# Four expert groups in turn, and the final norm of all rows under the last expert block

## The chip, the cores and the metric

One core of a Trainium2 chip runs the kernel. The metric is the device time of one execution in microseconds. Three runs of the kernel before gave 2179.16, 2179.3 and 2180.51, a median of 2179.3.

## The reference, cut to what matters

Two transformer-like blocks follow each other. What the change touches is the end of the second: a mixture of experts with 32 experts in 4 groups of 8, and the last norm.

```python
g_idx = argmax(g_logits)                       # one of 4 groups for each of 1024 tokens
top_val, top_loc = lax.top_k(e_logits, 2)      # two experts of that same group
expert = g_idx * 8 + top_loc
dest = pad_starts[expert] + rank               # sorted by expert, each padded to blocks of 128
out = (silu(xb @ w_gate[e]) * (xb @ w_up[e])) @ w_down[e]    # one block, one expert
y = zeros.at[slot_tok].add(out * slot_gate)    # rows go back to their tokens
x = x + gate_f * y
return rms_norm_2(x, final_g)                  # every row
```

Sums over experts may be made in any order, so the order of the blocks is free. Blocks of one expert never share a token; a token's two experts are always in one group.

## The kernel before, in words

The second block's residual rows lie in DRAM as `x3_dram`, the normed rows as `h4_dram`. Routing is worked out on VectorE (DVE, lines 1935 to 2070) with a few matmuls: one-hot vectors over 32 experts in `hot32`, their counts, slots, and for each block its expert (`bexp_u[:, 0]`), read by SyncE (SP) into a register when it loads weights. The last entry of `bexp` is the number of blocks beyond 32; its arrival raises `ov_known`. Blocks stand in the order of the experts, group after group.

Each block takes 12 weight chunks of 512 KB through a ring of 12 slots in SBUF. Matmuls are float32 made of three passes: ScalarE (ACT) copies a chunk to a rounded high part `mH`, DVE subtracts it from the chunk to get the low part `mL` (L2043 in the main loop, L2112 in the overflow blocks), and TensorE (PE) multiplies high by high, low by high and high by low (L2156, L2157, L2159). When a chunk's subtraction is done (`m2_lo`), its ring slot is free and SP loads the next block's chunk into it.

GpSimd (Pool) gathers a block's rows (L839, in the overflow blocks L906), and scatters the finished rows of the block before by an accumulating DMA into `x3_dram` (L850). A scatter waits until the scatter before has landed. The rows come out of PSUM by ACT, scaled by the slot's gate (L1305 and L1347), and Pool multiplies them by the modulation row `gate_ffn_row` (L844).

32 blocks are a fixed loop. The blocks beyond (here three) run in `overflow_blocks`: every engine walks 15 turns of a loop and skips the body where there is no block. In turn b the block 32 + b is computed, and the output of the block before it is weighed and scattered. In DVE's queue the body is: a small copy of row numbers (L2109), 12 subtractions (L2112), the hidden product (L2118), its low part (L2122), the low part of the next block's rows (L2127). PE waits for the hidden product's transposes before the down products.

Behind the loop the last block's rows are scaled by ACT (L1369), gated by Pool in two halves, and scattered. SP waits for that scatter (`last_out`), loads the 8 row tiles of `x3_dram` (L616), ACT squares them with a running sum (L1374), DVE makes the variance (L2134), Pool the power -0.5 (L935), DVE the scaled row times the final gain (L2139), and SP stores the tile (L619). Inputs go to `mH` and `mL`, squares and outputs to the ring.

Of the kernel before, what the change touches and what calls it, by code (L numbers as in the profile page):

```python
# [6 lines left out]
F32 = mybir.dt.float32  # L7
# [5 lines left out]
P = 128  # L13
D = 1024
# [20 lines left out]
    q_mm pm_ready pv hn_tr num_out final_in dve_steps cols_tr mod_mm xn_done  # L35
    tr_lo sums_out sums2_out sums_in row_cols row_tr row_copied rows_out rows_here c_here mid_tr tr_mid v_mm pool_steps neg_out mb_in mask_done exp_done small_ready small_exp sq_out intra_out kt_mm kw_out st_mm c_ready hd_out cell_w ov_l last_y last_out m2_row m2_dst rows_known aff_ready halves_out affT_tr m1_xT_lo m1_hid m1_hT_lo if_lo v_odd if_mm pool_mm k_mm k_out s_mm
    hn_ready q_out
# [46 lines left out]
def build(nc, ctx, io, out):  # L84
    def sb(name, shape, dt=F32, scope=ctx):
        return scope.enter_context(nc.sbuf_tensor(name, shape, dt))
# [104 lines left out]
    cnt_u = sb("cnt_u", [P, E2], U32, moe)  # L191
    bexp = sb("bexp", [P, NBLK + 1], scope=moe)
    bexp_u = sb("bexp_u", [P, 2, NBLK + 1], U32, moe)
    final_row = sb("final_row", [P, D], scope=moe)
# [50 lines left out]
    for name in SEMS.split():  # L245
# [5 lines left out]
        [("x1_done", NT), ("x1_done_2", NT)],  # L251
        [("sq2", NT), ("sq2_2", NT), ("sq_final", NT)],
        [("var2", NT), ("var2_2", NT), ("var_final", NT)],
        [("rstd2", NT), ("rstd2_2", NT), ("rstd_final", NT)],
        [("h2_out", 16 * NT), ("h2_out_2", 16 * NT)],
# [98 lines left out]
    def settle(eng):  # L354

        eng.sem_inc(S["wait_passed"])
# [55 lines left out]
    def m2_steps(eng, body):  # L412
# [6 lines left out]
        for s in range(E2 - 2, E2 + 1):  # L419
            body(s // 2, s % 2)  # L420

    def overflow_blocks(eng, overflow):
# [10 lines left out]
    one_rows = [ring[:, 2 * t, :] for t in range(6)] + [xz[:, 6, :], sg]  # L433
    two_rows = [ring[:, 2 * t + 1, :] for t in range(6)] + [xz[:, 7, :], hid]
    x_rows = [(mH, mL)[t // WSETS][:, t % WSETS, :].bitcast(F32) for t in range(NT)]
    row_at = [{}, {}]
# [15 lines left out]
    def _(sp):  # L452
# [157 lines left out]

        overflow_blocks(sp, overflow)


        sp.wait_ge(S["last_out"], 16)
        for t in range(NT):
            sp.dma_start(x_rows[t], x3_tiles[:, t, :]).then_inc(x_in[t], 16)  # L616
        for t in range(NT):
            sp.wait_ge(S["final_done"], t + 1)
            sp.dma_start(out.rearrange("(t p) d -> p t d", p=P)[:, t, :], one_rows[t]).then_inc(x_in[t], 16)  # L619
        for t in range(NT):  # L620
# [4 lines left out]
    def _(pool):  # L625
# [277 lines left out]
        def overflow(b):  # L903
            pool.wait_ge(S["ov_tok"], b + 1 + past["ov_tok"])
            settle(pool)
            pool.indirect_dma_start(out=xs[0], out_offset=None, in_=h4_dram,  # L906
                                    in_offset=bass.IndirectOffsetOnAxis(ap=otok[:, 0:1], axis=0),
                                    bounds_check=T - 1, oob_is_err=False).then_inc(xs_in[0], 16)
            pool.wait_ge(S["ov_y"], b + 1 + past["ov_y"])
            settle(pool)  # L910
            pool.wait_ge(m2_out[1], 16 * (E2 // 2 - 1) + XS_PAST)
            pool.wait_ge(m2_out[0], 16 * b + 16 * (E2 // 2) + XS_PAST)
# [5 lines left out]
            pool.wait_ge(S["m2_row"], 2 * b + 3 * (E2 - 1) + 2)  # L918
            settle(pool)
# [3 lines left out]
        pool.wait_ge(m2_out[1], 16 * (E2 // 2 - 1) + XS_PAST)  # L923
        pool.wait_ge(m2_out[0], 16 * blocks + 16 * (E2 // 2) + XS_PAST)
        settle(pool)
        pool.tensor_copy(last_tok[:], row_of[:, bass.ds(blocks + (E2 - 1), 1)]).then_inc(S["m2_row"], 1)
        for half in range(2):
            pool.wait_ge(S["last_y"], half + 1)
            gate_rows(ys[0], ys[0], slice(512 * half, 512 * half + 512))
        pool.wait_ge(S["m2_row"], 2 * blocks + 3 * (E2 - 1) + 3)  # L930
        settle(pool)
        scatter_rows(ys[0], last_tok).then_inc(S["last_out"], 16)
        for t in range(NT):
            pool.wait_ge(S["var_final"], t + 1 + past["var_final"])
            pool.tensor_tensor(stat[:, 10, t:t + 1], stat[:, 9, t:t + 1], neghalf[:, 0:1], ALU.pow).then_inc(S["rstd_final"], 1)  # L935


    @block.scalar
    def _(act):
# [399 lines left out]
        def overflow(b):  # L1339
            used, hi = past["m2_used"] + 12 * E2, past["m2_xT_hi"] + 2 * E2  # L1340
            for c in range(12):
                if c == 6:
                    act.wait_ge(S["m2_used"], 12 * b + used)
                    act.wait_ge(m2_out[1], 16 * (E2 // 2 - 1) + XS_PAST)
                    act.wait_ge(S["m2_row"], 2 * b + 3 * (E2 - 1))
                    settle(act)
                    act.activation(ys[1].rearrange("p (a b) -> p a b", a=2), ps[:, 4:6, :], ACT.Copy,  # L1347
                                   scale=slot_w[:, bass.ds(b + (E2 - 1), 1)]).then_inc(S["ov_y"], 1)
                if c == 9:
# [14 lines left out]
        blocks = overflow_blocks(act, overflow)  # L1364
        act.wait_ge(m2_out[0], 16 * (E2 // 2) + XS_PAST)
        act.wait_ge(S["m2_used"], 12 * blocks + 12 * E2 + past["m2_used"])
        settle(act)
        for half in range(2):
            act.activation(ys[0][:, 512 * half:512 * half + 512], ps[:, 4 + half, :], ACT.Copy,  # L1369
                           scale=slot_w[:, bass.ds(blocks + (E2 - 1), 1)]).then_inc(S["last_y"], 1)  # L1370

        for t in range(NT):
            act.wait_ge(x_in[t], 48)
            act.activation(two_rows[t], x_rows[t], ACT.Square,  # L1374
                           accum_out=stat[:, 8, t:t + 1]).then_inc(S["sq_final"], 1)


    @block.vector
    def _(dve):
# [724 lines left out]
        m2_steps(dve, m2_step)  # L2104

        def overflow(b):
# [22 lines left out]

        overflow_blocks(dve, overflow)  # L2130

        def variance(t):
            dve.wait_ge(S["sq_final"], t + 1 + past["sq_final"])
            dve.tensor_scalar(stat[:, 9, t:t + 1], stat[:, 8, t:t + 1], 1.0 / D, EPS, ALU.mult,  # L2134
                              ALU.add).then_inc(S["var_final"], 1)

        def finish(t):
            dve.wait_ge(S["rstd_final"], t + 1 + past["rstd_final"])
            dve.scalar_tensor_tensor(out=one_rows[t], in0=x_rows[t], scalar=stat[:, 10, t:t + 1], in1=final_row[:],  # L2139
                                     op0=ALU.mult, op1=ALU.mult).then_inc(S["final_done"], 1)  # L2140

        dve.wait_ge(S["final_in"], 16)
        for t in range(NT):
            variance(t)
            if t:
                finish(t - 1)
        finish(NT - 1)


# [567 lines left out]
```

## Time and profile before

| what | us |
|---|---|
| median of three runs | 2179.3 |
| the profiled execution's own time | 2180.93 |
| its span | 2179.3 |
| PE busy | 2030.7 (93%) |
| DVE busy | 1672.9 (77%) |
| ACT busy | 1240.9 (57%) |
| Pool busy | 467.9 (21%) |
| mean granted clock of PE | 0.973 |

The span is the time between the first and the last instruction of the profiled execution; the own time of that execution has what lies around the span too. An engine's busy time says how full it is, not whether it is what others wait for; for that one looks at what it waits for itself, and at the chain of work that ended last. The main expert loop of the second block lies between about 1505 and 2064 us, the three overflow blocks between 2064 and 2144, the last norm behind.

### The profile page before, as it was taken

What the parts mean: (1) busy time and instruction counts of PE and PEld (TensorE: products, weight loads), DVE (VectorE), ACT (ScalarE), POOL (GpSimd) and SP (SyncE); (2) the same over time, 40 slices, a digit from 0 to 9 for tenths busy, and PEclk for the clock granted to TensorE, in tenths of its full rate; (3) what the DMA queues carried; (4) which work ended last, traced back from release to release, by engine and by line L of the source; (5) the groups of instructions that cost most, each with busy time, mean ns of one, the idle gap of its engine ahead of it and who ended that gap; (6) DMA issues with size and microseconds to landing.
All of it is one profiled execution on the core that took longest, in us unless ns stands there. A gap on an engine that the chain in (4) does not pass through costs nothing.

```text
span 2179.3 us, 32240 instructions
## 1 busy us (share of the span) xinstructions
PE 2030.7 (93%) x9821; PEld 1685.3 (77%) x9821; DVE 1672.9 (77%) x1890; ACT 1240.9 (57%) x1460; POOL 467.9 (21%) x367
## 2 busy tenths in 40 slices
PE   3999999969999999999699999999999999999993
PEld 2888888857888878787577787888888888878872
DVE  5676755478999999999545455447999999999994
ACT  4311103207878787877533533223888888888873
POOL 2000001101011111111100353110344443433443
PEclk9999999959999999999899999999999999999997
DMA  9277754528999999999711112345999999999994
GB/s 344 89 249 242 244 189 165 198 102 317 381 378 389 380 387 381 386 382 385 262 44 47 41 39 106 126 174 192 395 382 383 376 370 379 377 374 365 367 333 155
DMA packets 234180, 592.47 MB, mean 272 GB/s; under 512 B 23938, under 2 KB 61078, under 8 KB 234108
## 3 DMA queue, kind: packets, MB, share of 16 engines
q1 hardware_dynamic: 207808, 518.06, 63.8%
q0 software_dynamic: 22640, 61.31, 9.6%
q10 hardware_dynamic: 3660, 12.17, 1.5%
q8 instruction: 42, 0.69, 0.1%
q14 instruction: 30, 0.25, 0.0%
HBM read 560.57 MB, written 50.91 MB: 281 GB/s over the span
## 4 chain that ended last, share of the span: by engine, by line
PE 50%; DMA 23%; DVE 11%; SPq 6%; issue 5%; ACT 3%; POOL 1%; ACTq 0%; DVEq 0%; POOLq 0%
PE ps L2156 15%; PE ps L2159 14%; PE ps L2157 14%; DMA ring<-in_w_expert_up 13%; DMA ring<-in_moe_w_down 7%; SPq L534 5%; DVE mL L2043 2%; DVE mL L1646 2%; DMA ring<-in_ada_w 1%; ACT mH L1292 1%; PE ps L2291 1%; PE ps L2435 1%; DVE xz L1792 1%; PE ps L2164 1%; PE ps L2253 1%
## 5 line engine op out<-in xcount | busy, mean ns | idle before, releaser
L2043 DVE TENSOR_TENSOR mL<-ring,mH 128x1024 fp32r<-128x1024 f32 x384 | 480.0, 1291 | 25.1 <-ACT mH L1292 24.4
L1646 DVE TENSOR_TENSOR mL<-ring,mH 128x1024 fp32r<-128x1024 f32 x384 | 454.8, 1222 | 33.8 <-ACT mH L1107 25.2
L1107 ACT ACTIVATE mH<-ring 128x1024 fp32r<-128x1024 f32 x384 | 402.2, 1063 | 100.8 <-PE ps L2159 61.2
L1292 ACT ACTIVATE mH<-ring 128x1024 fp32r<-128x1024 f32 x384 | 398.6, 1058 | 64.7 <-DMA ring<-in_w_expert_up 32.1
L2156 PE MATMUL ps<-mH,xsH 128*128 128x512 f32 x1072 | 428.7, 400 | 4.1 <-DVE mL L2043 2.4
L2159 PE MATMUL ps<-mH,xsL 128*128 128x512 f32 x1072 | 419.3, 391 | 0.0
L2157 PE MATMUL ps<-mL,xsH 128*128 128x512 f32 x1072 | 417.4, 389 | 0.0
L2156 PEld LDWEIGHTS ps<-mH,xsH 128*128 128x128 f32 x1072 | 201.6, 188 | 44.0 <-issue 3.3
L2159 PEld LDWEIGHTS ps<-mH,xsL 128*128 128x128 f32 x1072 | 201.2, 188 | 43.7
L2157 PEld LDWEIGHTS ps<-mL,xsH 128*128 128x128 f32 x1072 | 201.7, 188 | 38.7
L2156 PE MATMUL ps<-mH,hidH 128*128 128x512 f32 x536 | 213.6, 399 | 9.9 <-DVE hidL L1691 7.4
L844 POOL TENSOR_TENSOR xz<-xz,gate_ffn_row 128x340 f32<-128x340 f32 (+3 forms) x98 | 164.0, 1678 | 251.3 <-DVE mL L2043 210.3
L2157 PE MATMUL ps<-mL,hidH 128*128 128x512 f32 x536 | 209.7, 391 | 0.0
L2159 PE MATMUL ps<-mH,hidL 128*128 128x512 f32 x536 | 165.9, 391 | 0.0
L2156 PE MATMUL ps<-hH,wH 128*128 128x512 f32 x384 | 151.7, 395 | 3.8 <-DVE hL L1448 3.3
L2157 PE MATMUL ps<-hL,wH 128*128 128x512 f32 x384 | 150.0, 391 | 0.0
L2156 PEld LDWEIGHTS ps<-mH,hidH 128*128 128x128 f32 x536 | 100.9, 188 | 35.3 <-DVE mL L1646 11.3
L717 POOL DMA_INDIRECT xz<-h_dram,tok_in x16 | 42.8, 2675 | 376.8 <-DVE tok_in L1656 376.8
L1392 DVE SCALAR_TENSOR_TENSOR acc<-ring,silu_c,acc 128x1024 f32<-128x1024 f32 x83 | 106.6, 1284 | 22.1 <-DMA ring<-in_ada_w 15.1
L2159 PE MATMUL ps<-hH,wL 128*128 128x512 f32 x384 | 122.7, 391 | 0.0
L2159 PEld LDWEIGHTS ps<-mH,hidL 128*128 128x128 f32 x536 | 101.2, 189 | 21.8
L2157 PEld LDWEIGHTS ps<-mL,hidH 128*128 128x128 f32 x536 | 101.0, 188 | 19.5
(419 smaller groups left out, 3187.2 us busy)
## 6 DMA issues: line engine op xcount, KB each, us to landing
ring<-in_w_expert_gate SPq DMA_DIRECT2D x140, 512.0 KB
ring<-in_w_expert_up SPq DMA_DIRECT2D x140, 512.0 KB
ring<-in_w_expert_down SPq DMA_DIRECT2D x140, 512.0 KB
ring<-in_moe_w_gate SPq DMA_DIRECT2D x128, 512.0 KB
ring<-in_moe_w_up SPq DMA_DIRECT2D x128, 512.0 KB
ring<-in_moe_w_down SPq DMA_DIRECT2D x128, 512.0 KB
ring<-in_ada_w SPq DMA_DIRECT2D x96, 512.0 KB
ring<-in_sc_w_in SPq DMA_DIRECT2D x24, 512.0 KB
```

What stands on the lines that cost most here:

```text
L534: sp.dma_start(dst, src).then_inc(ring_in[s], 16)
L717: pool.indirect_dma_start(out=xs[r], out_offset=None, in_=h2_dram, in_offset=bass.IndirectOffsetOnAxis(ap=tok_in[r][:, 0:1], axis=0)).then ...
L844: pool.tensor_tensor(dst[:, at], src[:, at], gate_ffn_row[:, at], ALU.mult).then_inc(S["m2_row"], 1)
L1107: act.activation(mH[:, m % WSETS, :], ring[:, m % RING, :], ACT.Copy).then_inc(S["m1_hi"], 1)
L1292: act.activation(mH[:, wset, :], ring[:, slot, :], ACT.Copy).then_inc(S["m2_hi"], 1)
L1392: ins = dve.scalar_tensor_tensor(out=acc[:], in0=slot, scalar=silu_c[:, silu_col + k:silu_col + k + 1], in1=acc[:], op0=ALU.mult, op1=ALU.add)
L1646: dve.tensor_tensor(mL[:, m % WSETS, :], ring[:, m % RING, :], mH[:, m % WSETS, :].bitcast(F32), ALU.subtract).then_inc(S["m1_lo"], 1)
L1792: ins = dve.scalar_tensor_tensor(out=xz[:, i, back:T], in0=tA[:, 0:T - back], scalar=col("conv_w_2", 4 * (3 - back) + i), in1=xz[:, i, bac ...
L2043: dve.tensor_tensor(mL[:, wset, :], ring[:, slot, :], mH[:, wset, :].bitcast(F32), ALU.subtract).then_inc(S["m2_lo"], 1)
L2156: pe.matmul(o, high, rh, start=start, stop=False)
L2157: pe.matmul(o, high, rl, start=False, stop=False)
L2159: last = pe.matmul(o, low, rh, start=False, stop=stop)
```

## The change

It has four parts.

1. *Order of the blocks.* The one-hot vectors are written with a step of 4, so that place 4 * l + g holds expert l of group g. Four more DVE steps turn the place back into the expert's number, before `ov_known` is raised.
2. *Overflow blocks.* The weighing of the block before moves from ACT and Pool to one DVE instruction, ahead of the sixth subtraction. DVE then waits for `ov_sent`, a semaphore that Pool raises behind its scatter instruction. Pool no longer gates; it waits for the scatters before and scatters.
3. *Final norm of all rows under the last block.* SP waits for the scatter of the last block but one and for the ring slots of the last block, and then loads the 8 tiles of `x3_dram` to ring slots 0 to 7. Tiles are squared to ring slots 8 to 11, finished in place and stored as before.
4. *The last block's rows are patched in.* Pool gathers their rows of `x3_dram` (which lack the last block only); DVE weighs the last block's output and adds them; they pass the same norm as a ninth tile; when all eight stores have landed, Pool scatters these rows over `out`.

```diff
-                steps.mark(dve.tensor_tensor(hot32[:, i, :, 8 * g:8 * g + 8], hot8[:, i],
+                steps.mark(dve.tensor_tensor(hot32[:, i, :, bass.ds(g, 8, step=4)], hot8[:, i],
...
-        steps.mark(dve.tensor_copy(bexp_u[:, 0, 0:NBLK], bexp[:, 0:NBLK]))
+        step(dve.tensor_copy(bexp_u[:, 0, 0:NBLK], bexp[:, 0:NBLK]))
+        step(dve.tensor_scalar(bexp_u[:, 1, 0:NBLK], bexp_u[:, 0, 0:NBLK], 3, None, ALU.bitwise_and))
+        step(dve.tensor_copy(bgrp[:], bexp_u[:, 1, 0:NBLK]))
+        step(dve.scalar_tensor_tensor(out=bexp[:, 0:NBLK], in0=bgrp[:], scalar=31.0, in1=bexp[:, 0:NBLK], op0=ALU.mult,
+                                      op1=ALU.add))
+        steps.mark(dve.tensor_scalar(bexp_u[:, 0, 0:NBLK], bexp[:, 0:NBLK], 0.25, None, ALU.mult))
```

SP, behind the overflow blocks:

```diff
-        sp.wait_ge(S["last_out"], 16)
+        sp.wait_ge(m2_out[0], 16 * (E2 // 2) + XS_PAST)
+        sp.wait_ge(m2_out[1], 16 * blocks + 16 * (E2 // 2 - 1) + XS_PAST)
+        settle(sp)
         for t in range(NT):
+            sp.wait_ge(S["m2_lo"], 12 * blocks + 12 * (E2 - 1) + t + 1 + past["m2_lo"])
+            settle(sp)
             sp.dma_start(x_rows[t], x3_tiles[:, t, :]).then_inc(x_in[t], 16)
```

Pool, in each overflow block and behind them:

```diff
+            pool.wait_ge(m2_out[0], 16 * (E2 // 2) + XS_PAST)
+            pool.wait_ge(m2_out[1], 16 * b + 16 * (E2 // 2 - 1) + XS_PAST)
             settle(pool)
-            pool.wait_ge(S["m2_lo"], 12 * b + 12 * E2 + 11 + past["m2_lo"])
+            pool.wait_ge(S["m2_dst"], b + E2)
             settle(pool)
-            pool.tensor_copy(tok_out[0][:], row_of[:, bass.ds(b + (E2 - 1), 1)]).then_inc(S["m2_row"], 1)
-            gate_rows(gated, ys[1], slice(0, D))
-            scatter_rows(gated, tok_out[0]).then_inc(m2_out[0], 16)
+            scatter_rows(ys[1], tok_out[1]).then_inc(m2_out[1], 16)
+            pool.sem_inc(S["ov_sent"], 1)
...
+        pool.indirect_dma_start(out=last_base, out_offset=None, in_=x3_dram,
+                                in_offset=bass.IndirectOffsetOnAxis(ap=last_tok[:, 0:1], axis=0),
+                                bounds_check=T - 1, oob_is_err=False).then_inc(S["last_in"], 16)
+        for i in range(NT + 1):
+            pool.wait_ge(S["var_final"], i + 1 + past["var_final"])
+            own = stat_of(i)
+            pool.tensor_tensor(own[2], own[1], neghalf[:, 0:1], ALU.pow).then_inc(S["rstd_final"], 1)
         for t in range(NT):
+            pool.wait_ge(x_in[t], 64)
+        pool.wait_ge(S["last_done"], 1)
+        pool.indirect_dma_start(out=out, in_=last_rows, in_offset=None,
+                                out_offset=bass.IndirectOffsetOnAxis(ap=last_tok[:, 0:1], axis=0),
+                                bounds_check=T - 1, oob_is_err=False).then_inc(S["last_out"], 16)
```

DVE, in each overflow block (`weigh` is one instruction: PSUM times the slot's gate times `gate_ffn_row`) and behind them:

```diff
             for c in range(12):
+                if c == 5:
+                    dve.wait_ge(S["m2_used"], 12 * b + 12 * E2 + past["m2_used"])
+                    dve.wait_ge(m2_out[1], 16 * b + 16 * (E2 // 2 - 1) + XS_PAST)
+                    dve.tensor_copy(tok_out[1][:], row_of[:, bass.ds(b + (E2 - 1), 1)]).then_inc(S["m2_dst"], 1)
+                    weigh(ys[1], b + (E2 - 1)).then_inc(S["ov_y"], 1)
+                    dve.wait_ge(S["ov_sent"], b + 1)
...
+        def last_sum():
+            dve.wait_ge(S["m2_used"], 12 * blocks + 12 * E2 + past["m2_used"])
+            settle(dve)
+            dve.wait_ge(m2_out[0], 16 * (E2 // 2) + XS_PAST)
+            step(weigh(last_rows, blocks + (E2 - 1)))
+            dve.wait_ge(S["last_in"], 16)
+            dve.tensor_tensor(last_rows, last_rows, last_base, ALU.add).then_inc(S["last_y"], 1)
...
+        for i, t in enumerate(FINAL_ORDER):
+            if t == NT:
+                last_sum()
+            variance(i)
+            if i:
+                finish(i - 1)
+        finish(NT)
```

ACT loses the weighing in the overflow blocks and behind them, waits for the last block's subtractions, and squares nine tiles in place of eight.

## Rows read from the trace of the kernel before

**Rows 1.** Busy time by stretch: PE, PEld, DVE, ACT, Pool, then PE clock, DMA share, GB/s

```profile
1505.00:2064.00 559.00, 552.76 (x2598) 456.84 (x2599) 531.54 (x556) 470.38 (x528) 225.97 (x147) 1.00 1.01 378
2084.00:2144.00 60.00, 56.34 (x252) 45.57 (x252) 49.63 (x55) 41.39 (x50) 21.12 (x14) 0.97 0.62 225
2144.00:2179.30 35.30, 0.07 (x1) 0.00 (x0) 10.74 (x16) 10.46 (x18) 12.40 (x12) 0.55 0.63 238
...
2100.00:2102.00 2.00, 2.00 (x6) 1.55 (x5) 1.92 (x5) 2.00 (x3) 1.47 (x1) 0.50 1.03 412
...
2138.00:2150.00 12.00, 5.73 (x24) 4.42 (x24) 1.73 (x4) 2.17 (x4) 4.40 (x5) 0.90 0.03 4
...
2156.00:2177.00 21.00, 0.00 (x0) 0.00 (x0) 10.74 (x16) 9.20 (x16) 8.19 (x8) 0.50 1.01 389
```

**Rows 2.** Timeline of DVE in the routing: start, duration, engine, line, operation, [idle before]

```profile
1492.95 0.18 DVE L2025 TENSOR_SCALAR bexp<-bexp 128x47 f32<-128x47 f32 x1
1493.16 0.19 DVE L2026 CAST bexp_u<-bexp 128x47 uint32<-128x47 f32 x1
1493.26 0.15 DVE L2027 TENSOR_SCALAR bexp<-bexp 128x1 f32<-128x1 f32 x1
```

**Rows 3.** DVE instructions by form, whole span: count, then busy us and mean ns

```profile
L1668 DVE SCALAR_TENSOR_TENSOR xz<-ps,slot_gate,gate_ffn_row 128x1024 f32<-128x1024 f32 x16 | 20.4, 1274 | 0.0
```

**Rows 4.** Timeline of Pool: a scatter of the main loop, its last, the final one

```profile
2001.13 1.60 POOL L850 DMA_INDIRECT x_dram<-xz,tok_out  x1 [1.17 <-issue]
...
2085.61 1.64 POOL L850 DMA_INDIRECT x_dram<-xz,tok_out  x1 [0.90 <-POOL xz L844]
...
2150.34 1.59 POOL L850 DMA_INDIRECT x_dram<-xz,last_tok  x1 [0.90 <-POOL xz L844]
```

**Rows 5.** Semaphore instructions of Pool's queue between 2085 and 2088: ns, first to last

```profile
L356 POOLq EVENT_SEMAPHORE  x2: 17/17/17, 2086.6 to 2087.7; - x2
```

**Rows 6.** Timeline of DVE in the three overflow blocks

```profile
2082.05 15.10 DVE L2112 TENSOR_TENSOR mL<-ring,mH 128x1024 fp32r<-128x1024 f32 x12
...
2106.21 2.59 DVE L2112 TENSOR_TENSOR mL<-ring,mH 128x1024 fp32r<-128x1024 f32 x2 [0.16 <-ACT mH L1354]
...
2117.43 0.75 DVE L2118 TENSOR_TENSOR xz<-xz,ps 128x256 f32<-128x256 f32 x2 [0.44 <-PE ps L2159]
...
2121.07 6.90 DVE L2112 TENSOR_TENSOR mL<-ring,mH 128x1024 fp32r<-128x1024 f32 x6
...
2136.24 0.75 DVE L2118 TENSOR_TENSOR xz<-xz,ps 128x256 f32<-128x256 f32 x2 [0.45 <-PE ps L2159]
```

**Rows 7.** DMA issues (us to landing) from 2086, 2140, 2172; queue packets 2089 to 2092

```profile
xz<-h_dram,otok POOLq DMA_INDIRECT x1, 7.7
...
x_dram<-xz,last_tok POOLq DMA_INDIRECT x1, 4.1
...
out<-xz SPq DMA_DIRECT2D x2, 512.0 KB, 5.8
...
q0 software_dynamic: 139, 0.02, 5.2%
```

**Rows 8.** The overflow loop's branch on each queue, first and last of 15

```profile
L427 ACTq COMPARE_BRANCH  x15: 40/45/58, 2098.9 to 2144.6; - x15
...
L427 DVEq COMPARE_BRANCH  x15: 50/56/72, 2100.0 to 2145.5; - x15
```

**Rows 9.** Timeline of the final norm: SP, ACT, Pool, DVE

```profile
2154.50 0.82 SPq L616 DMA_DIRECT2D mH<-x_dram  x2
...
2157.77 1.06 ACT L1374 ACTIVATE ring<-mH 128x1024 f32<-128x1024 f32 x1 [11.61 <-DMA mH<-x_dram]
...
2159.26 0.57 POOL L935 TENSOR_TENSOR stat<-stat,neghalf 128x1 f32<-128x1 f32 x1 [7.33 <-DVE stat L2134]
...
2162.74 1.27 DVE L2139 SCALAR_TENSOR_TENSOR ring<-mH,stat,final_row 128x1024 f32<-128x1024 f32 x1
...
2170.47 2.48 DVE L2139 SCALAR_TENSOR_TENSOR xz<-mL,stat,final_row 128x1024 f32<-128x1024 f32 x2 [0.30 <-POOL stat L935]
```

More of the change, by code:

```diff
@@ L420, in m2_steps, with stat_of @@
             body(s // 2, s % 2)
+    FINAL_ORDER = list(range(NT + 1))
+    def stat_of(i):
+        return [stat[:, 8 + n, i:i + 1] if i < NT else stat[:, 11, n:n + 1] for n in range(3)]
     def overflow_blocks(eng, overflow):
@@ L430, in overflow_blocks @@
         return blocks
-    one_rows = [ring[:, 2 * t, :] for t in range(6)] + [xz[:, 6, :], sg]
-    two_rows = [ring[:, 2 * t + 1, :] for t in range(6)] + [xz[:, 7, :], hid]
-    x_rows = [(mH, mL)[t // WSETS][:, t % WSETS, :].bitcast(F32) for t in range(NT)]
+    x_rows = [ring[:, t, :] for t in range(NT)]
+    sq_rows = [ring[:, NT + u, :] for u in range(RING - NT)]
+    last_rows, last_base = ys[0], xz[:, 7, :]
     row_at = [{}, {}]
@@ L925, in _ @@
+        pool.wait_ge(m2_out[1], 16 * blocks + 16 * (E2 // 2 - 1) + XS_PAST)
         settle(pool)
[L926 to L930, printed above, removed]
-        settle(pool)
-        scatter_rows(ys[0], last_tok).then_inc(S["last_out"], 16)
@@ L938, in _ @@
+        pool.wait_ge(S["last_out"], 16)
     @block.scalar
@@ L1364, in _ @@
         blocks = overflow_blocks(act, overflow)
-        act.wait_ge(m2_out[0], 16 * (E2 // 2) + XS_PAST)
-        act.wait_ge(S["m2_used"], 12 * blocks + 12 * E2 + past["m2_used"])
+        act.wait_ge(S["m2_lo"], 12 * blocks + 12 * E2 + past["m2_lo"])
         settle(act)
[L1368 to L1375, printed above, removed]
+        for i, t in enumerate(FINAL_ORDER):
+            if i >= len(sq_rows):
+                act.wait_ge(S["sq_final"], i - len(sq_rows) + 1 + past["sq_final"])
+            if t < NT:
+                act.wait_ge(x_in[t], 48)
+            else:
+                act.wait_ge(S["last_y"], 1)
+            act.activation(sq_rows[i % len(sq_rows)], x_rows[t] if t < NT else last_rows, ACT.Square,
+                           accum_out=stat_of(i)[0]).then_inc(S["sq_final"], 1)
     @block.vector
@@ L2104, in _, with weigh @@
         m2_steps(dve, m2_step)
+        def weigh(dst, block):
+            return dve.scalar_tensor_tensor(out=dst.rearrange("p (a b) -> p a b", a=2), in0=ps[:, 4:6, :],
+                                            scalar=slot_w[:, bass.ds(block, 1)],
+                                            in1=gate_ffn_row[:].rearrange("p (a b) -> p a b", a=2),
+                                            op0=ALU.mult, op1=ALU.mult)
         def overflow(b):
@@ L2128, in overflow, with variance, finish @@
                                   part.bitcast(F32), ALU.subtract).then_inc(S["m2_xT_lo"], 1)
[L2130 to L2140, printed above, removed]
-        dve.wait_ge(S["final_in"], 16)
[L2143 to L2147, printed above, removed]
+        blocks = overflow_blocks(dve, overflow)
+        dve.tensor_copy(last_tok[:], row_of[:, bass.ds(blocks + (E2 - 1), 1)]).then_inc(S["m2_dst"], 1)
+        def last_sum():
[5 more added lines that the diff above has]
+            dve.tensor_tensor(last_rows, last_rows, last_base, ALU.add).then_inc(S["last_y"], 1)
+        def variance(i):
+            own = stat_of(i)
+            dve.wait_ge(S["sq_final"], i + 1 + past["sq_final"])
+            dve.tensor_scalar(own[1], own[0], 1.0 / D, EPS, ALU.mult, ALU.add).then_inc(S["var_final"], 1)
+        def finish(i):
+            t = FINAL_ORDER[i]
+            own, rows = stat_of(i), x_rows[t] if t < NT else last_rows
+            dve.wait_ge(S["rstd_final"], i + 1 + past["rstd_final"])
+            dve.scalar_tensor_tensor(out=rows, in0=rows, scalar=own[2], in1=final_row[:], op0=ALU.mult, op1=ALU.mult
+                                     ).then_inc(S["final_done" if t < NT else "last_done"], 1)
+        dve.wait_ge(S["final_in"], 16)
+        for i, t in enumerate(FINAL_ORDER):
+            if t == NT:
[4 more added lines that the diff above has]
+        finish(NT)
     @block.tensor
```

30 lines of the change are left out of this document (9 added, 21 removed).

## The prediction

> **What bounds the kernel now.** I read the page's slices first (PE is busy in nearly all of them, so only a stretch in which PE stands still can give much back), then the table by stretch, which shows where that is [rows 1], and last the timelines of single engines. Over the main expert loop (1505 to 2064 us) PE is busy 552.8 of 559 us at full clock, with the DMA engines at a share of 1.01: two limits at once. In the three overflow blocks (2084 to 2144) PE is still busy 56 of 60 us. From 2144 to the end PE does nothing for 35 us. That tail is a serial path: gating, a last scatter, loads of x3, final norm, stores. From 2156 to 2177 the DMA share is 1.01 again: 8 MB of loads and stores are what sets its pace, not the norm. So the change works on the right place: the 4 MB of loads can lie under the last block's products, where the DMA share is 0.03 (2138 to 2150 [rows 1]). What I weigh against it is what it puts on DVE in the overflow blocks and two more steps of DMA at the very end.
>
> **Routing, on the path.** The turn of the groups changes no number of blocks (the counts of the experts stay, 35 blocks) and no bytes. It adds to the DVE chain before the block table: today's copy to integers is issued 0.10 us before its successor [rows 2]; in its place stand four steps that wait for each other and one that doesn't. Successive waiting steps of this width start 0.21 us apart (1492.95 to 1493.16 [rows 2]), so 4 x 0.21 + 0.10 - 0.10 = 0.84 us. The `ov_known` increment and the copy of the first blocks' row numbers come right behind, then the first gather, so nothing hides it: **+0.85**. The eight strided one-hot products write as many elements as before; I cost them at nothing, since one element or 47 in a row make 0.15 or 0.19 us [rows 2], mostly fixed time; 0.04 more on each would be 0.3 us.
>
> **Overflow blocks.** Removed: ACT's scaled copy of the previous block's output, Pool's 2.4 us gating and its copy of row numbers. ACT and Pool are not on the path there. Added to DVE, between its fifth and sixth weight subtraction of each block: a small copy (0.15 us), the weighing (the same form, PSUM times a scalar times a row, is L1668: 1.27 us [rows 3]), and a wait for Pool's scatter. Seven subtractions of 1.14 us are queued behind it, and behind those the hidden product, which PE waits for.
> How long is the wait? Pool has to pass three small semaphore steps and issue the scatter. The engine starts a scatter 0.90 us after what released it [rows 4] in the case with one such step, 1.17 in the loop with three. The wait's release comes from Pool's queue, and the queue runs ahead of the engine: at 2086.6 it passed a semaphore instruction while the scatter of 2085.61 was still running for 1.64 us [rows 4, 5]. So the release comes at about the engine's start, not at its end. I take 1.1 us; bounds are 0.8 and 2.8 (0.9 to 1.2 plus the whole 1.6 us). Per block 0.15 + 1.27 + 1.1 = 2.5 us on DVE.
> What of it shows depends on DVE's slack:
> - First overflow block: DVE runs without a gap, 12 subtractions in 15.10 us from 2082.05 [rows 6]; no slack. It reaches the sixth at 2089.1 and has weighed at 2090.55. But Pool must also see that the scatter issued at 2085.61 has landed. Alone a scatter lands in 4.1 us; a gather under this load took 7.7 [rows 7]; between 2089 and 2092 the software queue moved 139 packets, about one scatter's 128 rows [rows 7]. So it lands near 2092.0 (bounds 2089.7 and 2093.3); release 0.9 later, 2092.9 in place of 2089.1: **+3.8**.
> - Second: the sixth subtraction ends at 2106.21 + 2.59 = 2108.8, six more take 6.8, so 2115.6, and the hidden product started at 2117.43, ended by PE [rows 6]. Slack 1.8; shown 2.5 - 1.8 = **+0.7**.
> - Third: 2121.07 + 6.90 = 2127.97, plus 6.8 is 2134.8, product at 2136.24 [rows 6]. Slack 1.45: **+1.05**.
> Sum +5.55. The bound turns from PE to DVE in all three.
> The granted clock was 0.50 from 2100 to 2102 [rows 1], at the down products of the first overflow block, after PE had been idle in front of them. I keep that one drop; PE will idle more now, and a second one would cost under 1 us, because DVE has become the limit.
> On the scatter and DVE together the Trainium skill (SBUF — State Buffer, Who interferes with whom) says that a two-input DVE instruction outside the two-port modes does not keep GpSimd from writing descriptors, but a two-port one locks it out until it ends. The scatter took 1.6 us beside running subtractions and 1.59 us with DVE idle [rows 4], so the trace agrees with the first half; by it the new wait protects nothing, and the sum carries its price without a gain.
>
> **Tail.** Each engine still walks the twelve unused turns of the overflow loop: ACT leaves at 2144.6, DVE at 2145.5 [rows 8]. From DVE's exit to the end is now 2179.3 - 2145.5 = 33.8 us. The new tail, counted from DVE's exit X:
> - x3 loads: SP waits for the last block but one's scatter (issued near 2134, landed near 2138 to 2139) and needs about 10.5 us for 4 MB at 389 GB/s [rows 1]: all in by X. Hidden under the last block's products. Without that cover they would cost up to 10 us.
> - DVE copies the last row numbers (X + 0.35), Pool's gather starts 0.9 later and holds Pool for some 1.15 us (my value, between nothing and the scatter's 1.59 [rows 4]): X + 2.4. The first power (0.57 [rows 9]) is queued behind it: X + 3.0. ACT has its first squares ready by then.
> - Eight tiles pass in the rhythm seen now: from the finish at 2162.74 to the end of the last at 2170.47 + 2.48 = 2172.95 seven take 10.2 us, 1.5 each [rows 9]. Seven are finished at X + 3.05 + 9.0 + 1.28 = X + 13.3.
> - Then the patch in series on DVE, ACT and DVE: weighing 1.35 with its wait, adding 1.25 (a two-input pass over as many elements as a subtraction), square 1.06 [rows 9] and about 0.2 to read its sum, variance 0.15: X + 17.35. PE's product has long been there.
> - The eighth tile's finish is behind that: X + 18.65. Its store is alone on the queues. Landing: a first load took from 2154.50 to 2157.77, 3.3 us; a store in the queue 5.8 [rows 7, 9]. I take 3.6: X + 22.3. The patched rows are finished earlier (X + 20.3).
> - Only now may Pool scatter the rows: 0.85 to start, 4.1 to land [rows 7], 0.5 to the end of the program (today the last store is issued near 2173.0, lands 5.8 later at 2178.8, and the span ends at 2179.3): X + 27.7.
> That is 33.8 - 27.7 = **-6.1**. The price of a single transfer is also on a page: the Trainium skill (DMA: Bandwidth & Descriptors, Anatomy of one DMA) puts some 2 us of fixed completion time on each DMA. By it the store would be an estimated 2 + 1.3 = 3.3 us, and the sum 0.3 lower.
>
> **Sum.** 0.85 + 5.55 - 6.1 = +0.3 us on the span of 2179.3. The profiled execution's own time is 2180.93, 1.6 above its span; the runs' median is 2179.3, so the forecast stands at **2179.6 us**. A measurement of this kernel can tell about 0.2%, 4.4 us, from nothing: I forecast no change, with gain and cost near 6 us each.
>
> **Rivals.**
> - *Slower, 2184.7:* DVE's wait lasts until the scatter's descriptors are written. Then each wait is 1.6 to 1.8 us longer, and as DVE is the limit all three show: +5.1. Against it the semaphore passed during a scatter [rows 5]; for it, that was another instruction's wait. It decides from about 1.3 us more per block on. Chance 0.15.
> - *Later, 2183.6:* the clock falls in all three blocks (two more at 0.9) and the last store lands in 5.8 us instead of 3.6 (+2.2). That is the edge of what can be told; chance 0.08, half of it beyond.
> - *Faster, 2174.5:* the scatter before lands early (2089.7: -2.3), the store in 3.3 us (-0.3), no clock drop comes (-0.9), and the tiles pass at DVE's own 1.28 us instead of 1.5, as no power is waited for (-1.6). Each is small; together they are what the block costs lean on. Chance 0.22.
> - *The order of experts moves the main loop:* with PE and DMA both full [rows 1], 1% of its 559 us is 5.6 us, either way. Nothing in the rows speaks for it, as bytes and blocks are the same. Chance 0.05.
> - *The loads are not hidden* (SP late): the tail keeps its DMA pace and only the block costs remain, 2185.7 and more. SP has no other work by then, and ring slots come free with the subtractions before 2140, so I give it 0.03.
>
> **The numbers.** The forecast has 0.47, with its own range 2175 to 2184. Faster by over 0.2% gets 0.24 (the faster rival and a share of the order's), slower 0.25 (the first slower rival, half the next, the unhidden loads and a share of the order's), and 0.51 lies within. Adding the rivals' places with a little room, the range is 2173 to 2187.
>
> **What would show it.** Right: the first overflow block some 4 us longer, the next two about 1 us; DVE's gap before the sixth subtraction near 1.1 us in the last two; loads of x3 landed before the first final square; DMA idle between single stores; about 28 us from DVE's loop exit to the end. Wrong: gaps near 3 us, a halved clock in several blocks, squares that wait for loads, or a first block that starts over 1 us later or earlier than 0.85 us behind today's.

## The result, and the profile after

The changed kernel runs at a median of 2184.3 us (2181.1 to 2186.3, 15 runs) beside 2179.6 us (2177.5 to 2183.5, 15 runs) for the kernel before on the same chip: ratio 1.0019, 95% interval 1.0013 to 1.0026. That is about 4.2 us slower, just inside the 0.2% that I had called no change, where 0.3 us had been forecast. The profiled execution took 2183.36 us by its own time, 2.4 more than that of before. Below, ratios of runs are turned into us of 2179.6; spans and steps come from single profiled executions. The interval of an experiment's ratio is some 2 us to each side, so where two experiments differ by less than about 3 us, the traces have to say what moved. Every ratio leaves slow runs out: there was one, of 5041.9 us, in the kernel without the wait for Pool.

The stretches of the kernel after, columns as in [rows 1]:

```profile
1505.00:2064.00 559.00, 554.79 (x2614) 459.89 (x2615) 534.88 (x558) 471.33 (x530) 230.64 (x148) 1.00 1.01 377
2081.00:2141.00 60.00, 51.13 (x224) 41.20 (x224) 50.38 (x56) 37.06 (x43) 14.07 (x8) 0.94 0.77 249
2141.00:2150.00 9.00, 8.08 (x28) 5.97 (x28) 2.46 (x6) 3.77 (x8) 0.00 (x0) 0.81 0.98 355
2150.00:2181.70 31.70, 0.06 (x1) 0.00 (x0) 14.48 (x21) 7.50 (x16) 10.84 (x11) 0.56 0.39 158
2093.00:2099.00 6.00, 4.76 (x11) 3.83 (x12) 6.00 (x6) 1.06 (x1) 2.59 (x1) 0.50 0.78 244
```

Beside [rows 1], PE is busy 2 us longer in the same 559 us of main loop (it has come further in them), but only 51 of 60 us in the overflow blocks, where it was 56. The loads of x3 now lie under the last block's products (DMA share 0.98 from 2141 to 2150, where it was 0.03), and the tail's DMA share has fallen to 0.39: both as forecast. The granted clock is 0.50, the lower of the two levels, from 2093 to 2099, behind PE's wait in the first overflow block.

DVE in the overflow blocks (the last column is the idle time ahead of an instruction and what ended it):

```profile
2078.88 0.14 DVE L2127 COPY otok<-row_of 128x1 uint32 x1
2086.07 1.27 DVE L2119 SCALAR_TENSOR_TENSOR xz<-ps,slot_w,gate_ffn_row 128x1024 f32<-128x1024 f32 x1
2092.96 8.04 DVE L2136 TENSOR_TENSOR mL<-ring,mH 128x1024 fp32r<-128x1024 f32 x7 [5.62 <-POOLq L928]
2101.11 0.75 DVE L2142 TENSOR_TENSOR xz<-xz,ps 128x256 f32<-128x256 f32 x2
...
2112.86 8.04 DVE L2136 TENSOR_TENSOR mL<-ring,mH 128x1024 fp32r<-128x1024 f32 x7 [1.07 <-ACT mH L1361]
2120.81 0.74 DVE L2142 TENSOR_TENSOR xz<-xz,ps 128x256 f32<-128x256 f32 x2
...
2132.72 8.04 DVE L2136 TENSOR_TENSOR mL<-ring,mH 128x1024 fp32r<-128x1024 f32 x7 [1.26 <-POOLq L928]
2140.67 0.75 DVE L2142 TENSOR_TENSOR xz<-xz,ps 128x256 f32<-128x256 f32 x2
```

The same hidden products stood at 2117.43 and 2136.24 in the second and third block of before [rows 6]. DVE's run into the first overflow block begins at 2078.9, 3.1 us earlier than the 2082.0 of [rows 6]; its first gap is 5.6 us, the other two 1.1 and 1.3.

The tail on DVE and Pool comes next, and then the end of the program. There each engine's queue closes with an instruction that the trace calls DRAIN; Pool's is the one to watch. (These lines come from the view of one line of the kernel: minimum, median and maximum in ns, then first and last start.)

```profile
2150.06 0.15 DVE L2155 COPY last_tok<-row_of 128x1 uint32 x1 [5.92 <-issue]
2152.86 1.28 DVE L2174 SCALAR_TENSOR_TENSOR ring<-ring,stat,final_row 128x1024 f32<-128x1024 f32 x1 [2.47 <-POOL stat L942]
...
2163.01 1.28 DVE L2119 SCALAR_TENSOR_TENSOR xz<-ps,slot_w,gate_ffn_row 128x1024 f32<-128x1024 f32 x1
2164.32 1.22 DVE L2163 TENSOR_TENSOR xz<-xz 128x1024 f32<-128x1024 f32 x1
...
2168.61 1.28 DVE L2174 SCALAR_TENSOR_TENSOR xz<-xz,stat,final_row 128x1024 f32<-128x1024 f32 x1 [0.44 <-POOL stat L942]
```

```profile
2171.79 1.05 POOL L946 DMA_INDIRECT out<-xz,last_tok  x1 [3.22 <-DMA out<-ring]
```

```profile
L80 SPq COMPARE_BRANCH  x1: 38/38/38, 2170.9 to 2170.9; - x1
L80 POOLq COMPARE_BRANCH  x1: 41/41/41, 2174.2 to 2174.2; - x1
L80 POOLq DRAIN  x1: 7096/7096/7096, 2174.4 to 2174.4; - x1
L80 SPq EVENT_SEMAPHORE  x1: 17/17/17, 2181.7 to 2181.7; - x1
```

The last data are in `out` by 2174.2 (the scatter landed 2.4 us after 2171.8), SP was done at 2170.9, and then all wait 7.1 us for Pool's drain. A drain counts as no busy time, so neither the busy table nor the timeline of Pool shows it. The kernel before had one too, hidden beside the last stores: it ended at 2170.2 + 7.8 = 2178.0, 0.9 us ahead of SP.

```profile
L80 POOLq DRAIN  x1: 7774/7774/7774, 2170.2 to 2170.2; - x1
L80 SPq COMPARE_BRANCH  x1: 38/38/38, 2178.9 to 2178.9; - x1
```

### The profile page after: what moved, and what is told of

The parts are those of the page before. It is cut to its first block, busy times and chain, and to the rows that moved or that the text cites. A ratio compares the mean times of both kernels' runs of the same rounds, so it can differ in the third digit from the quotient of the medians.

```text
span 2181.7 us, 32271 instructions
## 1 busy us (share of the span) xinstructions
PE 2032.7 (93%) x9821; PEld 1687.3 (77%) x9821; DVE 1681.4 (77%) x1905; ACT 1237.0 (57%) x1457; POOL 465.4 (21%) x360
## 4 chain that ended last, share of the span: by engine, by line
PE 56%; DMA 18%; DVE 11%; SPq 6%; issue 5%; ACT 3%; POOL 1%; DVEq 0%; ACTq 0%; POOLq 0%
PE ps L2193 16%; PE ps L2196 16%; PE ps L2194 16%; DMA ring<-in_w_expert_up 7%; DMA ring<-in_moe_w_down 7%; SPq L541 5%; DVE mL L1653 2%; DMA ring<-in_ada_w 1%; PE ps L2328 1%; DVE mL L2055 1%; PE ps L2472 1%; PE ps L2630 1%; DVE xz L1799 1%; PE ps L2201 1%; ACT mH L1306 1%
## 5 line engine op out<-in xcount | busy, mean ns | idle before, releaser
L855 POOL TENSOR_TENSOR xz<-xz,gate_ffn_row 128x340 f32<-128x340 f32 (+1 forms) x93 | 158.8, 1713 | 243.7 <-DVE mL L2055 215.4
```

Source lines behind the costliest of these rows:

```text
L855: pool.tensor_tensor(dst[:, at], src[:, at], gate_ffn_row[:, at], ALU.mult).then_inc(S["m2_row"], 1)
```

## Experiments

Each kernel is the changed kernel with one edit, unless said otherwise.

**The wait for Pool.** DVE doesn't wait for `ov_sent`, and Pool doesn't raise it.

```diff
-                    dve.wait_ge(S["ov_sent"], b + 1)
```

> The changed kernel without DVE's wait for Pool's scatter in the overflow blocks. Theory A (that wait is what the change loses: 5.6 us in the first block, because Pool itself waits for the big scatter of the block before, 1.1 and 1.3 in the next two): the gap before the sixth subtraction goes in all three blocks, the first block is 5.6 us shorter, the other two about 1 us in sum (PE's pace of 18.8 us per block takes over), so some 6.5 us less than the changed kernel: ratio to before near 0.999. Rival B (Pool's scatter is starved by DVE and its late landing stops something else: the next weighing, SP's loads of x3): the gap moves, the gain is under 2 us, ratio 1.001 to 1.002.

Ratio 0.9981 [0.9971, 0.9991], 8.3 us below the changed kernel; the three gaps of the trace of after sum to 5.62 + 1.07 + 1.26 = 7.95. The wait is all that the overflow blocks lost: from DVE's first `otok` copy to its loop exit it is 63.3 us here, 63.5 in before and 71.0 in the changed kernel. The wait's other side is seen in Pool's scatters of this kernel:

```profile
2093.84 3.66 POOL L861 DMA_INDIRECT x_dram<-xz,tok_out  x1 [7.19 <-issue]
...
2107.76 8.24 POOL L861 DMA_INDIRECT x_dram<-xz,tok_out  x1 [6.03 <-issue]
...
2126.84 8.05 POOL L861 DMA_INDIRECT x_dram<-xz,tok_out  x1 [6.22 <-issue]
```

With the wait each took 2.6 us, beside the same subtractions. So the wait does shorten the scatters, but little waits for them: the next one starts 14 to 19 us later, and only SP's loads of x3 stand behind the last. Those do start late, 4.1 us ahead of DVE's copy of the last row numbers, where it was 10.9 us in the changed kernel:

```profile
2138.96 5.15 SPq L627 DMA_DIRECT2D ring<-x_dram  x8
2143.07 0.15 DVE L2153 COPY last_tok<-row_of 128x1 uint32 x1 [5.91 <-issue]
```

ACT's first squares then wait for the loads. From that copy to DVE's weighing of the last block it is 14.8 us here, against 13.0 in the changed kernel and 13.3 to 13.8 in the three other kernels without the wait that finish these rows last. So for the 8 us that the wait costs in the blocks, it buys at most 0.4 to 1.8 us in the tail.

**What the first wait is for.** Pool no longer waits for the landing of block 30's scatter ahead of its scatter in the overflow blocks.

```diff
-            pool.wait_ge(m2_out[0], 16 * (E2 // 2) + XS_PAST)
```

> The changed kernel, but in the overflow blocks Pool no longer waits for the landing of block 30's scatter (blocks 30 and 31 share no token when groups take turns). Theory A (this landing is what makes the first of DVE's waits 5.6 us long): it becomes 1.1 to 1.3 us like the other two, 4.4 us less than the changed kernel, ratio near 1.000. Rival B (Pool comes late for another reason, its gather of 1.5 us or the queue): the wait stays over 4 us, ratio near 1.002.

Ratio 0.9997 [0.9988, 1.0007], 4.8 us below the changed kernel. The first gap is now like the others:

```profile
2090.70 8.04 DVE L2135 TENSOR_TENSOR mL<-ring,mH 128x1024 fp32r<-128x1024 f32 x7 [1.20 <-POOLq L927]
```

5.62 - 1.20 = 4.4 us of the first gap were this landing.

**The order of the blocks.** Two kernels: the changed one with blocks in the old order (`hot32` and the table as before; its edit is shown), and the kernel before with the new order alone (the same edit the other way round):

```diff
-                steps.mark(dve.tensor_tensor(hot32[:, i, :, bass.ds(g, 8, step=4)], hot8[:, i],
+                steps.mark(dve.tensor_tensor(hot32[:, i, :, 8 * g:8 * g + 8], hot8[:, i],
```

> The changed kernel with the blocks in the old order (group after group), all else as changed. Theory A (the order changes only which block stands where: in the old order block 30 has few rows, its scatter lands some 3 us sooner after its issue, so DVE's first wait is 2.5 to 3 us instead of 5.6; routing 0.4 us shorter): 3 us less than the changed kernel, ratio near 1.0005. Rival B (the order of the groups speeds up the main loop, which was 3.1 us shorter in the profile after): the main loop gets these 3 us back and the time is that of the changed kernel, ratio near 1.002.

> The kernel before with the order of the groups alone changed (first of the change's four parts). Theory A (the turns keep the weights ahead of PE longer; the main loop from the row-number copy of block 0 to that of block 30 takes 537 to 538 us with them in four profiles, 540.0 without in two, and the way into the overflow blocks 0.8 less): routing +0.4, loop and entry -3.4, so 3 us less than before, ratio 0.9986. Rival B (the difference of these profiles is chance or comes with other parts of the change): ratio 1.0002, loop at 540.

Without turns 1.0026 [1.0016, 1.0036], 1.5 us above the changed kernel; turns alone 0.9986 [0.9977, 0.9995], 3.0 us below before. The first met neither theory fully, and by its ratio alone it could not be told from the changed kernel. By its trace both effects are there, with opposite signs. Its first gap fell to 3.91 us (1.7 less), and its main loop took 2.2 us longer. From the first copy of a block's row numbers to the one of block 30 it is 540.0 us, as in before, and 537.8 in the changed kernel. In the kernel with turns alone it is 537.1.

To tell the rows from the weights, the rows stand in the old order and the weights in that of the turns (the experts' weights are then not those of the rows):

```diff
-                steps.mark(dve.tensor_tensor(hot32[:, i, :, bass.ds(g, 8, step=4)], hot8[:, i],
+                steps.mark(dve.tensor_tensor(hot32[:, i, :, 8 * g:8 * g + 8], hot8[:, i],
```

(only this line; the table of experts stays changed.)

> The changed kernel with rows in the old order but the weights read in the order of the turns, so each block is multiplied by another expert's weights (the result is not the reference's). It asks which half of the turns matters. Theory A (which rows stand in a block: group by group the gathers and scatters are uneven, and DMA falls behind): the loop stays at 540 us as without the turns, ratio near 1.0026. Rival B (the addresses from which the weights come): the loop takes 537 to 538 us, ratio near 1.001.

Ratio 1.0022 [1.0012, 1.0031]: by itself it doesn't tell the two theories apart. Its loop does: 541.1 us, so the order of the weights gives nothing. Over all traces the old order of rows took 540.0, 540.0 and 541.1 us, the new one 536.6 to 538.6 us in eleven kernels. The view of the DMA queues shows what else changed: packets, MB and share of the 16 engines of Pool's queue, first from 1505 to 2064 us in before, with turns off, and with weights alone (15.96 MB in all three), then in the changed kernel, and last from 2064 to 2145 in before and in the changed kernel.

```profile
q0 software_dynamic: 8640, 15.96, 11.8%
```

```profile
q0 software_dynamic: 8640, 14.69, 11.0%
```

```profile
q0 software_dynamic: 1152, 0.19, 1.8%
```

```profile
q0 software_dynamic: 1152, 1.46, 10.7%
```

1.27 MB of gathered and scattered rows leave the main loop, whose DMA share is 1.01, and come back behind it, where the share was 0.62 [rows 1]. In the old order the last blocks carry few rows, with turns many more. At the loop's 377 GB/s 1.27 MB are 3.4 us; the loops with turns are 1.4 to 3.4 us shorter than 540.0. So the size fits, but no run moved the bytes by themselves: that they are the cause is argued and not shown. The same fuller block makes the scatter of block 30 slower: Pool saw it landed 9.4 us after its issue (2082.49), without turns 7.7.

**The end of the program.** SP and not Pool waits for the last scatter:

```diff
+        sp.wait_ge(S["last_out"], 16)
...
-        pool.wait_ge(S["last_out"], 16)
```

> The changed kernel, but SP waits for the last scatter to land and Pool ends with its issue. Theory A (Pool's closing drain of 7.1 us runs from Pool's own last instruction and is the last thing of all): the drain starts at the end of the issue instead of at the landing, about 1.4 us earlier, and still takes 7.1: 1.4 us less, ratio near 1.0013. Rival B (the drain waits for something of the DMA): it becomes longer by the same 1.4 us, no change of the time.

Ratio 1.0009 [1.0000, 1.0019], 2.2 us below the changed kernel, with intervals that overlap. The trace settles it: from the start of the scatter to the end of the drain it is 8.2 us, where it was 9.7, so 1.5 us are gained, the 1.4 of theory A. Pool's queue comes to the drain just before the scatter starts on the engine (2170.82), and the drain ends 7.1 us after the scatter (2171.87 + 7.1 = 2179.0), so it is longer without costing more:

```profile
L80 POOLq DRAIN  x1: 8384/8384/8384, 2170.6 to 2170.6; - x1
```

Next, without the scatter over `out` and Pool's waits ahead of it (the last block's rows then lack that block):

```diff
-        for t in range(NT):
-            pool.wait_ge(x_in[t], 64)
-        pool.wait_ge(S["last_done"], 1)
-        pool.indirect_dma_start(out=out, in_=last_rows, in_offset=None,
...
-        pool.wait_ge(S["last_out"], 16)
```

> The changed kernel without its last scatter and Pool's waits in front of it: the rows of the last block are not written over the output (left out), all else is there. Theory A (the drain comes with any end of Pool): Pool drains from its ninth power, 2168.6 + 7.1 = 2175.7, later than SP's last landing at 2170.8: 6 us less than the changed kernel, ratio near 0.999. Rival B (the drain of 7 us belongs to the scatter just before it): the end follows the last store, 10 us less, ratio near 0.9972.

Ratio 0.9987 [0.9977, 0.9997], 7.0 us less. Even so Pool sets the end, not SP, whose last store landed at 2171.7:

```profile
L80 POOLq DRAIN  x1: 8597/8597/8597, 2167.9 to 2167.9; - x1
```

Its last power ends at 2169.5, and the drain 7.0 us later. So the 7 us do not come from the last scatter, as theory A had it.

**Is the drain fixed?** The two edits that gained, together (no wait for Pool, SP at the end):

> The changed kernel without DVE's wait for the scatter, and with SP instead of Pool waiting for the last landing. Theory A (the two costs are independent: 8.3 us and 1.4 to 2.2 us in the runs of each alone): 10 us less than the changed kernel, ratio to before 0.9970 to 0.9975. Rival B (the starved scatters of 8 us delay Pool or the loads of x3 once the end is shorter): ratio 0.998, no better than without the wait alone.

Ratio 0.9976 [0.9967, 0.9985]: faster than both kernels. To this a drain of Pool ahead of its ninth power was added:

```diff
+            if i == NT:
+                pool.drain()
```

> The kernel after without DVE's wait for Pool and with SP waiting for the last scatter (which ran at a ratio of 0.9976), and a drain of Pool put ahead of its ninth power, where Pool stands still for 3.56 us (2155.99 to 2159.55 in that kernel's trace). Theory A: the closing drain's 7.1 us run anew from Pool's last instruction, whatever was drained before; the early one then holds the ninth power until 2155.99 + 7.1 = 2163.1, 3.5 us later, of which some 2.5 us reach the last scatter (it waits for the stores anyway): ratio 0.9987. Theory B: it is work left by earlier instructions, done once; the early drain takes it, the closing one is short (1 to 2 us), and the end comes 2.5 us later and 5 to 6 us earlier: ratio 0.9960 to 0.9965. Theory C: only the closing drain is long, the early one costs under 1 us and changes nothing: ratio 0.9976.

Ratio 0.9963 [0.9950, 0.9977], in the range of theory B. Its interval overlaps that of the kernel without the drain, and again the trace decides. The early drain lasted until 2165.6. DVE had the ninth variance at 2161.90, and without a drain the power starts 0.23 us after it, so it was held up by 3.6 us (I had written 3.5):

```profile
2161.90 0.15 DVE L2168 TENSOR_SCALAR stat<-stat 128x1 f32<-128x1 f32 x1 [1.27 <-ACT ring L1382]
2165.71 0.55 POOL L944 TENSOR_TENSOR stat<-stat,neghalf 128x1 f32<-128x1 f32 x1 [7.14 <-issue]
```

But the closing drain was short:

```profile
L80 POOLq DRAIN  x1: 2740/2740/2740, 2168.3 to 2168.3; - x1
```

It began with the scatter still ahead of it (2168.51, 1.05 us), so 1.5 us of it lie behind that. The last block's rows as third of the nine tiles instead, without a drain:

```diff
-    FINAL_ORDER = list(range(NT + 1))
+    FINAL_ORDER = [0, 1, NT] + list(range(2, NT))
```

> The same faster kernel, with the last block's rows as third of the nine tiles and not as ninth. Theory A (the end is a serial path of DVE, last store, last scatter, closing drain): weighing, adding and the square of these rows move to where DVE stood idle for 2.81 us or runs beside the other tiles; the eighth tile's finish moves from 2159.39 to about 2158.0, the gap of 1.28 us before it being gone, but not the 2.5 us of weighing and adding: 1.0 to 1.5 us earlier, ratio 0.9969 to 0.9972. Rival: the gather of the rows (issued 2143.3, landed about 2146) and the product's end hold up the second finish and all behind it, so that nothing is gained: ratio 0.9976 or above.

Ratio 0.9999 [0.9990, 1.0008], 5 us worse than without: the rival, and more than it said. The gather, issued at 2144.6 among the loads of x3, took 7.0 us to land. DVE waited for it, and then for ACT's square of the sum, with seven tiles behind:

```profile
2151.72 1.23 DVE L2161 TENSOR_TENSOR xz<-xz 128x1024 f32<-128x1024 f32 x1 [2.15 <-DMA xz<-x_dram,last_tok]
2154.15 0.15 DVE L2166 TENSOR_SCALAR stat<-stat 128x1 f32<-128x1 f32 x1 [1.21 <-ACT ring L1380]
```

**The drain where Pool has time.** Between the third block's scatter and the gather of the last rows Pool stands still for 15.8 us. First in the changed kernel, then in the faster one:

```diff
         blocks = overflow_blocks(pool, overflow)
+        pool.drain()
```

> The changed kernel with a drain of Pool as it leaves the overflow loop; from the third block's scatter (ends 2135.4) to the gather of the last rows (2151.16) Pool stands still for 15.75 us, so 7.1 us of drain lie in the open there. Theory A: the closing drain's length is work that has piled up over the kernel, taken by the first drain: the closing one is down to 1 to 2 us, the end 5 to 6 us earlier, but not before SP's end (last store landed 2170.8, Pool's landing 2174.2): span about 2176, ratio 0.9993 to 0.9997. Theory B: it comes from what Pool did last (its powers and the gather of the tail): the closing drain keeps 7.1 us, ratio 1.0019. A length between tells how much of it the tail's own nine powers and one gather make.

> The same drain in the faster kernel (without DVE's wait, SP waiting for the last scatter; ratio 0.9976). Theory A: closing drain 1 to 2 us after the last scatter's 1.05, so the end is set by that scatter's landing near 2167 and not by 2172.4: 4.5 to 5 us earlier, ratio 0.9953 to 0.9957, below the 0.9963 of the drain before the ninth power, which held that power up. Theory B: unchanged, 0.9976.

Ratios 0.9989 [0.9980, 0.9998] and 0.9955 [0.9942, 0.9969]: one line takes 6.5 us from the changed kernel, and the other version, 2170.0 us, is 9.8 us below before. In the trace of the first the early drain ran from 2140.1 for 6.9 us, with nothing waiting for it, and the closing one is short:

```profile
L931 POOLq DRAIN  x1: 6932/6932/6932, 2140.1 to 2140.1; - x1
...
L80 POOLq DRAIN  x1: 214/214/214, 2174.4 to 2174.4; - x1
```

In the changed kernel the closing one took 7096 ns in the same place. The rest of that timeline hardly moves: the last scatter is issued at 2171.80 there, at 2171.79 in the changed kernel. In the second kernel the closing drain is 2.8 us, nearly half of it beside the scatter:

```profile
L80 POOLq DRAIN  x1: 2793/2793/2793, 2166.1 to 2166.1; - x1
```

## Why the prediction was nearly right in time, and wrong in its steps

No change was forecast, and the time lies within its range; but the sum was +0.3 us where the ratio says +4.2 and the profiled executions +2.4. Two errors made the forecast too fast, by 4.1 us (tail) and 3.4 us (first block); three made it too slow, by 3.1 (main loop), 1.4 (second block) and 0.4 us (routing). That they mostly cancelled, and that the number came out near, is luck. In the profiled executions, step by step:

| step | forecast | measured | from |
|---|---|---|---|
| ahead of the block table | 0 | -0.4 | its first reduction starts at 1490.74, not 1491.12; the spread of single executions |
| routing | +0.85 | +0.42 | from the table's integer copy to the copy of the first row numbers 1.27 us, not 0.85 |
| main loop | 0 | -3.1 | overflow starts at 2078.9, not 2082.0; block 0's row numbers copied at 1534.9 in both |
| first block | +3.8 | +7.15 | gap of 5.6 us |
| second block | +0.7 | -0.7 | gap 1.1 |
| third block | +1.05 | +1.05 | gap 1.3 |
| tail | -6.1 | -2.0 | DVE's loop exit at 2149.9 to 2181.7 is 31.8 us |
| sum | +0.3 | +2.4 | |

- **"0.5 to the end of the program"** is the step that failed most. I took it from SP's end in before and left Pool's closing drain out, since Pool had been done early there. A wait on Pool for the last scatter puts all of the drain's 7.1 us behind everything else. The drain moved ahead gives 6.5 us back, and the rest of that kernel's timeline stays as it was.
- **The first block's wait** had the right mechanism (landing of the scatter before) and the wrong size. The forecast meant a gap of 2.35 us (weighing done at 2090.55, release at 2092.9), and a landing 6.4 us after the issue. 1.7 us of the miss are the turns, which put a fuller block in place 30; the other 1.6 are mostly a landing of 7.7 us even without them (gap 3.91). I had taken the 139 packets [rows 7] for one scatter's rows, though the block's gather was in the same queue, and hadn't asked how full the block is once the order changes.
- **Routing, "so nothing hides it":** the added steps took 0.91 us, for the 0.84 I gave them, but before had 0.41 us of idle time on DVE ahead of the copy of the first row numbers, and that hid half:

```profile
1494.01 0.15 DVE L2033 CAST tokc<-ps 128x2 uint32<-128x2 f32 x1 [0.41 <-issue]
```

  The other half shows: the step is 0.85 us in the changed kernel without turns too, and 1.26 with turns alone. It is not seen in the start of block 0 because the profiled execution of the changed kernel was 0.4 us ahead by then.
- **"Nothing in the rows speaks for it"**, of the order of experts, was another failed step: a chance of 0.05 for what gave 3.0 us by itself (turns alone). Blocks and weights stay the same, the rows don't: the DMA view by stretch shows 15.96 MB in the loop and 0.19 MB behind it. I had asked only whether bytes are added, not where they go; beside the full stretch (1.01) lies one with room (0.62 [rows 1]). That the bytes are the reason fits in size and is not shown.
- **The drop of the clock** was kept in the first block; it moved with PE's wait (0.50 from 2093 to 2099) and lies in the stretch that is lost anyway. The -0.7 of the second block is the drop that before had at 2100 to 2102 [rows 1], gone from there. What such a drop costs is seen from the hidden product of the first block to that of the second: 20.4 us with it (before, and the kernel with the drain ahead of the ninth power, clock 0.57 from 2098 to 2102); without it 19.4 us in the kernel with turns alone and 18.75 to 18.85 us in the four other kernels without the wait for Pool (clock 1.00 there). So one drop cost 1.0 to 1.6 us, where I had written 0.9. Near 2144 a second one came, under the last products, and the DVE copy that ends the loop does not wait for PE.
- **Waits of 1.1 us, not 2.8:** right. The rival in which DVE waits until descriptors are written forecast 2184.7, near the 2184.3 that came; its mechanism is refuted: the semaphore was raised at 2092.82, the scatter began at 2093.05 and ran until 2095.6, and DVE's next subtraction began at 2092.96.
- **"The new wait protects nothing"** leaned on a page (the Trainium skill, SBUF — State Buffer, Who interferes with whom), by which such a DVE instruction does not keep GpSimd from writing descriptors, but does contend with a GpSimd instruction that reads SBUF; I had used the first half only. The traces lie between: without the wait 14 of 15 scatters took 3.1 to 8.25 us beside the run of subtractions, and ended only behind it, while one took 2.56, those of the main loop take 1.6 [rows 4], and gathers beside the same subtractions 1.3 to 1.5. So the wait does protect the scatter, but what that is worth is at most 0.4 to 1.8 us in the tail.
- **The tail up to the patched rows** was right to 0.3 us (finished at 2169.9, which is DVE's exit + 20.0, where + 20.3 was forecast). The store landed in 2.6 us for 3.6, and the scatter in 2.4 for 4.1, which I had read from the scatter of [rows 7]. With the start of the scatter this made the data complete 3.0 us earlier than forecast, and hid part of the drain in the sum. The page's figure for a single transfer (the Trainium skill, DMA: Bandwidth & Descriptors, Anatomy of one DMA), an estimated 3.3 us, was nearer to the store, and still above it; that section is on transfers which GpSimd issues, and this store is SP's.

What stays open: what Pool's first drain works off, as one at 2140 took 6.9 us with Pool idle since 2135.4, and a later one after eleven more instructions 0.2; why one of the scatters beside subtractions was quick, and those of the main loop; and whether the moved bytes are what shortened the main loop.

## What to carry to other kernels

Read, for each engine, when its last instruction ends and what the program's closing instructions cost it: work that is put behind an idle engine also moves its drain behind everything, and an early drain in idle time can take that off the path. An order of work that leaves all totals alone still decides which stretch carries the bytes; look for the full one and its neighbour. A new wait costs what its releaser is itself waiting for: follow the chain one step further (the scatter before, and how full its block is). Add the misses up by step: a sum near the measured time does not show that its terms are right.

## What the runs showed of the hardware that was not expected

- Pool's first drain ends about 7 us after the instruction ahead of it, or after its own start where Pool is idle by then (7.0 to 7.15 in every kernel without an early drain, 6.9 to 7.6 for the three early ones); a later one ends 0.2 us after its start on an idle Pool, or 1.5 us after the scatter ahead of it.
- An increment of a semaphore that stands behind an indirect DMA in Pool's queue passed 0.23 us before that DMA began, and 2.8 us before it ended.
- Transfers with the queues nearly empty, in the changed kernel: 2.6 us for a store of 512 KB, 2.4 us for the last scatter (144 packets, 0.01 MB), 2.8 us for the gather of the last rows, which took 7.0 us among the loads of x3 in the experiment on the order of tiles.
- The granted clock fell to 0.57 from 2098 to 2102, behind PE's short waits at the first hidden product, in one of the five kernels without the wait for Pool, and stayed at 1.00 in the other four with the same code there; the block with the drop took 1.5 us longer.
